# Scale before shift in the first modulation, q on the scaled tokens, and another plan for the running sums of the adaLN vectors

## What is computed

```python
mod = jax.nn.silu(cond) @ p['w_ada'][l] + p['b_ada'][l]
sh1, sc1, gt1, sh2, sc2, gt2 = jnp.split(mod[:, None, :], 6, axis=-1)
h = _rmsnorm(x, p['g_pre_mix'][l]) * (1.0 + sc1) + sh1
...
proj = h @ p['w_in'][l]        # q, k, v, g, low-rank decays, Hyena inputs
# gated linear attention in 4 heads, forward and backward, chunks of 64 tokens
# Hyena: short conv, then two gated long convolutions with filters made by a small MLP
y = jnp.concatenate([y_gla, y_hy], axis=-1) @ p['w_out'][l]
x = x + gt1 * _rmsnorm(y, p['g_post_mix'][l])
h = _rmsnorm(x, p['g_pre_ffn'][l]) * (1.0 + sc2) + sh2
y = _moe(h, l, p)              # 16 experts in 4 groups, top 2 in the best group
x = x + gt2 * _rmsnorm(y, p['g_post_ffn'][l])
```

## Time and profile before

| | |
|---|---|
| median of 3 runs | 1530.67 us (1525.83 to 1532.94) |
| the profiled execution's own time | 1527.67 us |
| its span, first to last instruction | 1525.9 us |
| mean granted TensorE clock | 0.963 |
| PE busy | 1383.1 us (91%), 5198 instructions |
| DVE busy | 749.1 us (49%), 1272 instructions |
| ACT busy | 241.9 us (16%) |
| DMA | 422.19 MB, mean 277 GB/s |

### The profile page before, as it was taken

One profiled execution on the slowest core, in us unless ns is written; L12 is line 12 of the kernel. 1 busy time (PEld: TensorE's weight loads), 2 busy tenths in 40 slices (PEclk: granted clock), 3 DMA queues, 4 the chain that ended last, 5 costly groups with the idle time before them and its releaser, 6 DMA issues.

```text
span 1525.9 us, 14046 instructions
## 1 busy us (share of the span) xinstructions
PE 1383.1 (91%) x5198; PEld 631.0 (41%) x5198; DVE 749.1 (49%) x1272; ACT 241.9 (16%) x401; POOL 75.1 (5%) x126
## 2 busy tenths in 40 slices
PE   2679999999999989999999999889989897898977
PEld 0135544444555545555544444533333333333322
DVE  0138888998677687978693752530000000000006
ACT  2110320100011011211121101421110111111104
POOL 3010000000001000000000001000000000000001
PEclk9699999999999999999999999999999999999999
DMA  9997558777549652322215854599999999999997
GB/s 347 423 382 240 178 170 277 255 254 241 165 163 334 213 154 104 111 73 87 83 55 196 297 168 170 221 360 427 427 428 399 427 427 428 427 391 428 427 425 283
DMA packets 134032, 422.19 MB, mean 277 GB/s; under 512 B 10253, under 2 KB 76024, under 8 KB 116852
## 3 DMA queue, kind: packets, MB, share of 16 engines
q1 hardware_dynamic: 120292, 375.79, 64.5%
q0 software_dynamic: 7584, 33.38, 6.0%
q10 hardware_dynamic: 6096, 12.20, 2.1%
HBM read 407.96 MB, written 22.58 MB: 282 GB/s over the span
## 4 chain that ended last, share of the span: by engine, by line
PE 72%; DMA 13%; DVE 9%; issue 3%; ACT 2%; ACTq 0%; SPq 0%; DVEq 0%
PE ps L506 19%; PE ps L503 16%; PE ps L895 13%; DMA s_mem<-in_w_exp_gate 8%; PE ps L915 7%; DMA s_mem<-in_w_ada 4%; PE ps L777 3%; DVE s_mem L1597 2%; DVE s_mem L1771 2%; PE ps L450 2%; PE ps L674 1%; DMA s_mem<-in_hy_freq 1%; PE ps L625 1%; PE ps L432 1%; DVE s_mem L1743 1%
## 5 line engine op out<-in xcount | busy, mean ns | idle before, releaser
L1597 DVE SCALAR_TENSOR_TENSOR s_mem<-s_mem,s_sT 128x512 f32<-128x512 f32 x480 | 339.4, 748 | 33.8 <-DMA s_mem<-in_w_ada 17.2
L503 PE MATMUL ps<-s_mem 128*128 128x384 f32 x1024 | 342.4, 492 | 1.2 <-DMA s_mem<-in_w_in 1.2
L506 PE MATMUL ps<-s_mem 128*128 128x512 f32 x672 | 294.9, 598 | 0.7 <-ACT s_mem L1372 0.7
L895 PE MATMUL ps<-s_mem 128*64 128x512 f32 x1152 | 257.0, 603 | 16.3 <-DMA s_mem<-in_w_exp_gate 15.6
L503 PEld LDWEIGHTS ps<-s_mem 128*128 128x128 f32 x1024 | 193.2, 191 | 142.7 <-issue 17.1
L506 PEld LDWEIGHTS ps<-s_mem 128*128 128x128 f32 x672 | 127.1, 191 | 159.9 <-issue 158.8
L895 PEld LDWEIGHTS ps<-s_mem 128*64 128x64 f32 x1152 | 85.9, 139 | 183.8 <-issue 182.7
L2071 DVE TENSOR_TENSOR s_mem<-s_mem,ps 64x512 f32<-64x512 f32 x18 | 12.2, 679 | 293.4 <-ACT s_mem L1464 293.4
L915 PE MATMUL ps<-s_mem 128*64 128x512 f32 x576 | 147.3, 671 | 9.3 <-DVE s_mem L2073 9.3
L915 PEld LDWEIGHTS ps<-s_mem 128*64 128x64 f32 x576 | 44.4, 153 | 98.9 <-issue 87.1
L1268 ACT ACTIVATE s_mem<-ps 128x512 f32<-128x512 f32 (+1 forms) x61 | 34.4, 580 | 316.3 <-PE ps L506 154.0
(11 more groups left out here) (292 smaller groups left out, 1025.6 us busy)
## 6 DMA issues: line engine op xcount, KB each, us to landing
s_mem<-in_w_ada SPq DMA_DIRECT2D x256, 256.0 KB, 3.3
s_mem<-in_w_exp_gate SPq DMA_DIRECT2D x32, 2048.0 KB, 21.9
s_mem<-in_w_exp_up SPq DMA_DIRECT2D x32, 2048.0 KB, 23.1
s_mem<-in_w_exp_down SPq DMA_DIRECT2D x32, 2048.0 KB, 24.2
s_mem<-in_w_in SPq DMA_DIRECT2D x24, 2048.0 KB, 9.3
s_mem<-in_w_ada SPq DMA_DIRECT2D x16, 2048.0 KB, 11.6
s_mem<-in_w_out SPq DMA_DIRECT2D x8, 2048.0 KB, 8.0
y_slots<-s_mem ACTq DMA_DIRECT2D x34, 256.0 KB
```

The lines of the kernel that those rows point to most:

```text
L503: m = mm(ps[:, banks[m_], 0:TOK], v[:, k, m_ * P:(m_ + 1) * P], hT[:, kk, :], start=(kk == 0), stop=(kk == KT - 1))
L506: m = mm(ps[:, banks[m_], :], hT[:, kk, m_ * P:(m_ + 1) * P], v[:, k, :], start=(kk == 0), stop=(kk == KT - 1))
L895: m = mm(ps[half, 0, :], hgT[:, kh * 8 + k, :], weights(e, 2 * kh + which)[:, k, :], start=(kh + k == 0), stop=(kh * 8 + k == KT - 1), ski ...
L1597: v.op(ve.scalar_tensor_tensor(out=o, in0=w, scalar=scale, in1=o, op0=ALU.mult, op1=ALU.add), S("piece_used") if last else None)
```

## The change

**Scale first.** The scale block of `w_ada` is loaded ahead of the shift block. `scale_step` takes 1024 columns (half a vector) and 512 rows in each 2 MB load; two half vectors of four steps each. ACT copies the sums out, PE turns them into columns and adds partial sums with a table of ones (`scale_columns`, `conds`), and DVE scales eight blocks of `hT` (`scale_tokens`), first the lower half, then the upper half.

**q on scaled tokens.** q's weights get places of their own (`wq`) and are loaded among the scale and shift loads (`Q_LOAD_AFTER`). PE multiplies them with the scaled tokens while the upper scale and the shift block are loaded. What the shift adds to q is the same for all tokens of a condition: it is computed apart, as shift times q's weights (16 matmuls, `qshift`, then `q_shift_columns`), and ACT adds it as a bias when it copies q out. DVE adds the shift to `hT` (32 instructions at L1752) once q has read it. A fourth 2 MB slot (slot 3) exists for the first 16 loads, over a region used later.

**Order of the rest.** k's first half comes ahead of `lr`; the `la` products stand between the quarters of k's second half. Small loads go ahead of the first `w_ada` load, and the tokens ahead of the small filter tables on ACT's queue.

**Running sums.** Half steps: 110 ahead of the heads instead of 136, 47 in the heads instead of 44, 29 after them instead of 20; `filter_sums` gets 2 more ahead of L1761's successor (now L1885), and 2 stand between `long_conv` and `gate_conv` of filters 1 to 3; then 8 as before, 10 new ones behind the last `gate_conv`, and 22 in the output projection instead of 32. The sums move with them.

The diff, cut:

```diff
-        ADA_SUMS = {("q", 1): 0, ("k", 1): 1, ("v0", 1): 2, ("v1", 0): 3, ("v1", 1): 4, ("g0", 0): 5, ("g0", 1): 6,
+        ADA_SUMS = {("v0", 0): 0, ("v0", 1): 1, ("v1", 0): 2, ("g0", 0): 3, ("g0", 1): 4, ("g1", 0): 5, ("g1", 1): 6,
...
+            def scale_step(h, r):
+                cols = SCALE * D + 2 * h * NCOL
+                w = next_slot(pe, w_ada[4 * r * P:4 * (r + 1) * P, cols:cols + 2 * NCOL].rearrange("(k p) n -> p k n", p=P))
+                for kk in range(4):
+                    k = 4 * r + kk
+                    for jj in range(2):
+                        j = 2 * jj + k % 2
+                        m = mm(ps[32 * j:32 * j + 32, 7 - h, :], sT[:, k, :], w[:, 2 * kk + jj, :], start=(k < 2),
+                               stop=(k >= KT - 2), skip_group_check=True)
...
+            pe.wait_ge(S("in_q0"), 16)
+            for m_ in range(4):
+                take(pe, m_, f"q_{m_}", ("act",))
+                m = q_products(m_, range(8))
+                scale_step(1, m_)
+            m.then_inc(S("q_read"), 1)
+            shift_step(0)
+            scale_columns(1)
+            shift_step(1)
...
+            for m_ in range(2):
+                q_products(m_, range(12, KT)).then_inc(filled(f"q_{m_}"), 1)
+                shift_step(4 + m_)
+            shift_step(6)
+            shift_step(7)
+            q_products(2, range(12, KT)).then_inc(filled("q_2"), 1)
+            wait_read(pe, "dve", "shift")
+            mod_columns(SHIFT, 5)
+            q_products(3, range(12, KT)).then_inc(filled("q_3"), 1)
...
+            for k in range(KT):
+                j = k % 4
+                m = mm(ps[32 * j:32 * j + 32, 6, :], sT[:, k, :], wq[k // 8][:, k % 8, :], start=(k < 4),
+                       stop=(k >= KT - 4), skip_group_check=True)
+            m.then_inc(filled("qshift"), 1)
...
-            project("q", "fm", w_in, COL_Q)
+            where_k = ("k", "fm", w_in, COL_K)
+            project_half(*where_k, 0, between=q_shift_columns, banks=(4, 5, 7, 0))
...
+            project_half(*where_k, 1, banks=(4, 5, 7, 0), turn=decay_products())
...
             for kt in range(KT):
+                if kt in (0, 8):
+                    dve.wait_ge(S("q_read"), kt // 8 + 1)
+                if kt == 12:
+                    dve.wait_ge(filled("q_3"), uses["q_3"][2])
+                for c, toks in both:
+                    v.op(ve.tensor_scalar(hT[:, kt, toks], hT[:, kt, toks], sT[:, kt, 2 + c:3 + c], None, ALU.add),
+                         S("h_shifted") if c == 1 else None)
-            run(26)
+            run(17)
...
+                    if h % 2 == 1 and (d, h) != (1, 3):
+                        run(3)
-            run(4)
+            run(6)
...
-                    run((2, 1, 2, 1, 1, 1, 2, 2)[event])
+                    run((2, 2, 2, 1, 1, 1, 2, 2)[event])
...
+                meanwhile(2)
...
-                meanwhile()
+                meanwhile(4)
...
-            run(7)
-            mod_chunk(11)
-            run(8)
+            run(10)
+            mod_chunk(10)
+            run(10)
...
+                    run(2)
                     gate_conv(ho - 1)
-                filter_sums(ho, lambda: run(4))
+                filter_sums(ho, run)
```

More of the change, by code:

```diff
@@ L77, in shape_constants @@
     lower = (np.arange(P) >= BLK)[:, None]
-    base = np.concatenate([ident, tri, sel.reshape(P, 2 * P), total, np.tile(rows, (P, 1)), tokens, lower], 1).astype(np.float32)
+    shifts = np.zeros((P, 32), np.float32)
+    for j in range(4):
+        for c in range(2):
+            shifts[32 * j + 2 + c, c] = 1
+    conds = np.zeros((P, 2, 32), np.float32)
+    for j in range(4):
+        for c in range(2):
+            conds[32 * j + c, j // 2, c] = 1
+    base = np.concatenate([ident, tri, sel.reshape(P, 2 * P), total, np.tile(rows, (P, 1)), tokens, lower, shifts, conds.reshape(P, 64)], 1).astype(np.float32)
     masks = np.zeros((P, 2, P), np.int32)
@@ L480, in mod_columns, with scale_columns @@
                 m.then_inc(filled(f"modT{q}"), 1)
-            wait_read(pe, "dve", ADA_KEYS[0])
-            mod_columns(0, 2)
-            pe.wait_ge(S("mod_ready"), 1)
-            mod_columns(1, 3)
+            def scale_columns(h):
+                wait_read(pe, "act", f"scale{h}")
+                take(pe, 5, f"scaleT{h}")
+                for i in range(8):
+                    m = mm(ps[:, 5, 32 * i:32 * i + 32], scale_sums[:, i % 4 * P:(i % 4 + 1) * P], conds[:, i // 4, :],
+                           start=True, stop=True, skip_group_check=True)
+                m.then_inc(filled(f"scaleT{h}"), 1)
@@ new lines, in q_products @@
+            def q_products(m_, kts):
+                for kt in kts:
+                    if m_ == 0:
+                        pe.wait_ge(S("h_scaled"), kt + 1)
+                    m = mm(ps[:, m_, 0:TOK], wq[kt // 8][:, kt % 8, m_ * P:(m_ + 1) * P], hT[:, kt, :],
+                           start=(kt == 0), stop=(kt == KT - 1))
+                return m
+            pe.wait_ge(S("sT_ready"), 2)
+            scale_step(0, 0)
+            scale_step(0, 1)
+            pe.wait_ge(S("x_scaled"), NT)
@@ new lines, in _ @@
+            for kt in range(KT):
+                x_turn(kt)
+                if kt in (4, 9):
+                    scale_step(0, 2 + kt // 9)
+            scale_columns(0)
+            pe.wait_ge(S("in_rowsB"), 32)
+            take(pe, 4, "colB")
+            tr(ps[:, 4, 0:96], rowsB, ident[0:96, 0:96]).then_inc(filled("colB"), 1)
+            pe.wait_ge(S("in_mlp"), 16 * 9)
+            take(pe, 3, "hid1")
+            mm(ps[0:HID, 3, 0:TOK], w1s, pe_sb, start=True, stop=True).then_inc(filled("hid1"), 1)
@@ L487, in project_half, with q_shift_columns @@
+            def q_shift_columns():
+                wait_read(pe, "act", "qshift")
+                take(pe, 6, "colQ", ("act",))
+                for m_ in range(4):
+                    m = mm(ps[:, 6, m_ * 32:m_ * 32 + 32], q_shift[:, m_ * P:(m_ + 1) * P], shift_rows, start=True,
+                           stop=True, skip_group_check=True)
+                m.then_inc(filled("colQ"), 1)
             def project_half(key, kind, w, col0, kh, readers=("act",), between=None, banks=(0, 1, 2, 3),
@@ L495, in project_half @@
                         take(pe, banks[m_], bk, readers)
-                    if m_ == 2 and between:
+                    if m_ == (1 if key == "k" else 2) and between:
                         between()
@@ L1218, in load @@
                 act.dma_start(dst, src).then_inc(S(sem), 16)
+            for t in range(NT):
+                load(x_sb[:, t, :], x_rows[t], f"in_x{t}")
             load(rowsB[0:72, :], T["hy_conv_w"][0].rearrange("j (m p) -> (j m) p", p=P), "in_rowsB")
@@ L1228, in _ @@
                 load(dst, src, "in_mlp")
-            for t in range(NT):
-                load(x_sb[:, t, :], x_rows[t], "in_x")
             wait_read(act, "dve", "colA")
@@ new lines, in _ @@
+            inverse_roots(0, NT)
+            for t in range(NT):
+                v.op(ve.tensor_scalar(h_tm[:, t, :], x_sb[:, t, :], stat[:, t:t + 1], None, ALU.mult), S("x_scaled"))
+            scale_tokens(0)
+            b = read(dve, "colB")
+            v.op(ve.tensor_copy(colB[:, :], ps[:, b, 0:96]), freed("dve", "colB"))
+            dve.wait_ge(S("in_mlp"), 16 * 9)
+            sine_argument("hid1", 0, HID)
+            scale_tokens(1)
+            sine_argument("hid2", 1, P)
+            dve.wait_ge(S("in_rows"), 16 * 8)
@@ L1653, in _ @@
             mod_chunk(0)
-            run(14)
+            run(16)
             wait_read(dve, "act", "q_3")
```

269 lines of the change are left out of this document (144 added, 125 removed).

## The result

The changed kernel takes 1512.7 us (median of 4 runs, 1511.34 to 1514.97), against 1529.6 us for the one before in the same comparison (4 runs, 1525.83 to 1532.94): a ratio of 0.9897, with a 95% interval of 0.9881 to 0.9912. It is 16.9 us faster. The profiled execution took 1513.4 us, with a span of 1511.6.

The account below looks back on a forecast made before the run. Transfers bound the start until 97 us, then PE, if DVE lets it run. 28.8 - 1.0 - 1.0 - 4.9 - 0.3 + 1.2 = 22.8 us gained gave 1507 us, range 1496 to 1520.

Parts of the forecast that it names:

- Start: From the first loads to v0: q overlaps the loads, so v0 starts at 172.8 instead of 201.6, gaining 28.8 us.
- The 11.8 us for the loads: Start: q's two loads cost 10.8 us, changed run lengths 1 more, putting the last shift product at 109.0.
- From v0 to the heads: Stretch ahead of the heads: DVE, with 26 fewer half steps, is ready just about early enough; 1.0 us charged.
- an event ahead of which DVE waits: nothing: Heads: one half step more in three heads falls where DVE waits anyway and costs nothing.
- the 1.0 for two sums: First head to output projection: two more sums on PE, 0.99 us each, one absorbed by a stall; 1.0 us charged.
- the piece wait goes: Behind the heads: DVE's 5.5 us wait for a piece disappears, as the new plan issues those pieces before the load.
- Behind the heads: From last head to first tap: nine more half steps put the tap's reading at +59.8 instead of +54.9, losing 4.9 us.
- Filter blocks: Half steps ahead of each norm's input and gate_conv are covered by DVE's existing waits; 0.3 us charged in all.
- Output projection: Ten half steps move into a DVE wait, so PE's 1.24 us for chunk 14 go; gain 1.2 us.
- (b): Rival, start: PE's q matmuls between scale products run at lower clock and fall behind; 1526 or 1515 us, chance 0.11.
- (c): Rival: waits for pieces return around the heads and DVE comes late in four blocks; 13.5 us, 1521, chance 0.07.
- (d): Rival, slower: the 26 half steps moved behind the heads' start are uncovered and cost 38.4 us; 1540, chance 0.04.

Follow-up runs that it names:

- sixth run: The changed kernel with all 64 q matmuls placed behind the last shift product, loads and slots unchanged; 1547.26 us, ratio 1.0133.
- seventh run: The changed kernel with 52 more VectorE instructions ahead of the heads, about as much as the 26 half steps taken from there; 1544.99 us, ratio 1.0114.
- eighth run: The changed kernel with first and third run's edits, one more half step in heads 1 to 3, sum 10 earlier, two half steps moved later; 1504.85 us.
- first run: The changed kernel with GpSimd's 6.3 MB HBM-to-HBM copy of the tokens moved behind the second filter; 1506.58 us, ratio 0.9856.
- third run: The changed kernel with a 2 MB load issued one piece earlier (one piece less behind load 28, one more behind 29); 1506.82 us, ratio 0.9857.
- fifth run: The changed kernel without the instructions of nine half steps behind the heads, pieces still loaded; read up to the expert loop, which starts at 987.34 us.
- fourth run: The changed kernel without the instructions of the 14 half steps added in the filter blocks, pieces still loaded; 1532.72 us, readable only up to the expert loop.

## Why the prediction was right, and where 6 us went

- **Start, 28.8 us predicted.** Right in what gains: q runs under the loads (sixth run). The last shift product began at 111.01 (predicted 109.0), k at 123.88 (121.6), v0 at 174.40 instead of 201.64: 27.2 us. That the last shift product is only 2.0 us off is partly luck, for two errors work against each other. The 11.8 us for the loads are too much: from 24 to 96 us, with most of q's two loads and the other run lengths in it, the engines moved 410 GB/s at full share, and not the 322 of the upper end; with PE out of the way (sixth run) the last product began at 107.15, 10.0 behind the 97.16 of before (one profile of each). And the sum had no term for what holds the last loads back: they wait for slots that PE releases, and PE had work without a break until 108.19 (predicted 106). That adds 3.9 us. Behind the last load 12.9 us were needed, 12.6 predicted, although the product itself ran at a granted clock of 0.54 and took 3.45 us.
- **From v0 to the heads, 1.0 charged.** Nothing was lost that shows: DVE waited 3.07 us for PE ahead of its first head instruction. The seventh run shows that this margin was all there was.
- **Heads: "an event ahead of which DVE waits: nothing", and the 1.0 for two sums.** Here is the step that failed: the sum put the waits for pieces in the heads at nothing. The half steps themselves are free there (three more cost nothing in the eighth run). The stretch cost 6.78 us. One sum more fits 0.9 (the first run takes 126.16 against 125.27). The other 5.9 are the piece wait, and the first and third run each bring them back. I had followed pieces only behind the heads ("the piece wait goes") and reasoned from the number of pieces ahead of a load. There it was right: DVE waits for no piece from the last head to the tap. But the same plan put the load 5.6 us later in the heads, onto the copy and DVE's need of a piece. The copy I had not looked at. PE's 4.39 us behind it are the sign that the prediction named for being wrong, a wait for DVE of more than 3 us away from the tap. The second sum cost its 1.1 us in the filter blocks, and neither fell into a stall: 2 us instead of 1.
- **Behind the heads, 4.9 lost.** Measured 5.06, the tap at +59.98 against +59.8. The fifth run takes the nine half steps out and gets 3.7 of it; the other 1.3 are mostly the sum more on PE. The wait for the tap is 8.19, not near 10; the rest of it is the 1.28 ahead of the sum.
- **Filter blocks, 0.3.** The half steps cost 0.1 (fourth run), covered by the waits of the earlier trace rows. Those ahead of `gate_conv` are not nearly gone, as forecast, but fell from 18.8 to 6.7 us.
- **Output projection, gain 1.2.** It didn't come. PE's 1.24 us ahead of running sum 14 stand in the changed kernel and in every other run. A shorter queue on DVE didn't move them, so DVE's lateness wasn't from the half steps that I took away. What sets it was not tried.
- **Rivals.** (b) fell, but for the first eight q matmuls, which took 7.09 us (granted clock 0.72 from 46 to 52 us); the other groups between the scale products ran at 5.43 us for eight, 0.68 each, at a granted clock of 1.00. Of (c), the returning piece wait is what happened, though in another place and at 6 us, not 13.5. (d) is far off, but the sixth run shows how it would have looked without the overlap: 18.8 us slower.

Taken together, by the profiled pair up to the expert loop: 22.8 us predicted; less 0.6 up to DVE's first head instruction (27.24 for 27.8); less 6.8 in the heads and filter blocks (8.10 lost, 1.3 charged for their half steps and sums); less 0.1 behind the heads; plus 1.75 behind the blocks, which is the scatter of the clock. That makes 17.05, and 17.06 were measured. The close fit of the start's row is that of one pair of profiles; the other profile of before would put it 3.9 us above the forecast.

## What to carry to other kernels

When a plan of loads changes, follow every queue that feeds a consumer through all of the program: what matters is which other transfers, from any engine's queue, fall into the same 30 us as its need, and not only how many were issued ahead. A transfer that costs nothing at its place beside one plan (the HBM-to-HBM copy before: no difference when moved) can cost 6 us at the same place beside another. And when work is moved in between loads, look at what releases the buffers: here the last loads waited for PE, and the sum that counted only bytes came out right by two errors. And a kernel with data-dependent work can't be timed with part of its arithmetic left out; such runs are read by landmarks up to that point.

## What the runs showed of the hardware

A copy of 6.3 MB from HBM to HBM held 70.8% of the time of the 16 DMA engines for 26 us and with it the landing of 256 KB transfers on another queue took 20.3 us (median), against 3.1 without it. That queue's transfers held 30.1% of the engines' time beside the copy and 39.7% without it.

PE's granted clock behind short waits differed between runs of one program. The last shift product (16 records; the windows catch one more) in the changed kernel and in the fifth run:

```profile
111.00:114.40 3.40, 3.39 (x17) 0.60 (x17) 0.00 (x0) 0.00 (x0) 0.00 (x0) 0.54 1.04 401
```

```profile
111.10:113.00 1.90, 1.90 (x17) 0.47 (x17) 0.00 (x0) 0.00 (x0) 0.00 (x0) 1.00 1.02 391
```

A granted clock of 0.54 is nearly all at 1.2 GHz, 1.00 is 2.4. PE had waited 2.82 and 2.24 us for its load before. In the third run it took 2.60 us behind a wait of 2.19, so the wait alone doesn't decide it. In the other runs it took 1.92 us behind waits of 1.35 and 1.51, and 3.09 to 3.59 behind waits of 2.45 to 2.78. The difference, 1.5 us, is as large as the errors of the start's terms.
